# Attention scores and sums over keys as products of high and low fp32r parts, with query parts stacked on 128 rows

## The chip, the cores and the metric

The program runs on one core of one Trainium2 chip. The metric is the device time in microseconds (us), the median over runs. A core has the engines TensorE (PE; its weight loads are shown as PEld), VectorE (DVE), ScalarE (ACT), GpSimd (POOL) and SyncE (SP, which issues DMAs). Each takes its instructions in the order in which the program wrote them, and they meet at semaphores.

## What is computed

A diffusion block on 512 tokens and 256 context tokens of width 1024, then a second block with retention, gated linear attention and a product-key expert layer. The change touches the attention of the first block: 8 query heads over 2 key-value heads of width 64, for 512 queries and 768 keys (256 of them from the context).

```python
q, k, v, gb, gc, u = split_heads(px, q_norm[l], k_norm[l])      # rmsnorm of each head of q and k
a = latent_attention(apply_rope(q, cos, sin), apply_rope(k, cos, sin), v, kc, vc)
sc = gb * short_conv3(gc * u, conv_w[l])
mix = jnp.concatenate([rmsnorm(a, attn_out_norm[l]), rmsnorm(sc, conv_out_norm[l])], axis=-1)

def gqa_softmax(q, k, v):
    s = jnp.einsum('bqkgd,bskd->bkgqs', q, k, preferred_element_type=jnp.float32) * ATTN_SCALE
    p = jax.nn.softmax(s, axis=-1).astype(v.dtype)
    return jnp.einsum('bkgqs,bskd->bqkgd', p, v)
```

## The kernel before

Each engine has one hand-written list of steps, and this order by hand is the schedule; no planner stands behind it. PE writes into a ring of double banks of PSUM (`acc`) in numbered units. `begin(u)` waits until unit u-2 was freed, and ACT or DVE free a unit when they have read it (`acc_free`). Weights come in tiles of 128 x 1024: SP loads them, ACT copies out the high part (`high_part`, called through `ahead`), POOL subtracts (L2184), and each product of the projections is three fp32r products, high with high, high with low, low with high (L533 to L539). The attention of before doesn't do that: its products are plain fp32, and each shows as two matmul records in the trace.

**The projections of the mixing layer (L661 to L711).** PE computes q, k, v, then four tiles `gb`, four `gc`, four `u`, of 24 products of 512 columns each. Between the gate tiles lie the steps that make q and k ready: `stat` (L478, the mean of squares of each head, `blk64`), `rotated(t)` (L673, waits for `normed`, swaps pairs for the rotary embedding), `doubled_keys` (L680) and `to_tokens` (L658, v turned to tokens). For tile t, ACT squares, takes logarithm and exponential (`inverse`, each with a table load) to give `rstd`; DVE scales (L1728, `normed`), and after `rotated(t)` adds the rotary terms (`rope`, L1720 to L1722, `copied`). DVE does tile t wholly before tile t+1. ACT copies each gate tile out of PSUM (`gates`), so that a step which stands behind a `gates` in ACT's list can't begin before PE has finished that tile.

**The attention loop (L750 to L760; ACT L1254 to L1274; DVE L1751 to L1772).** A unit u is one head and 128 queries; there are 32. In step s PE does `scores(s+1)` (L724), `turn(s-2)` (L736, six transposes of the probabilities of a unit) and, every fourth step, `outputs(h)` (a product for the 512 queries of one head, shown as L478 into `misc`). ACT does the exponential of unit s with its row sum, then copies half of the turned unit s-3. DVE does the reciprocal of the sum of unit s-1 (L1756), scales that unit's probabilities (L1758), takes the row maximum of unit s (L1762) and its negative (L1763), and copies the other half of unit s-3 (L1771). Before a unit's exponential ACT needs DVE's L1763; before DVE's L1756 it needs the exponential. After the loop ACT and DVE norm the result and split it for the product with `w_mix_out`. POOL has nothing to do in the loop.

## Time and profile before

| what | us |
|---|---|
| median of 3 runs (3372.78 to 3380.73) | 3378.37 |
| profiled execution, its own time | 3377.58 |
| its span, first to last instruction | 3375.8 |
| PE busy in the span | 2841.4 (84%) |
| DVE, ACT, POOL busy | 1671.4, 951.1, 1072.3 |
| projections of the mixing layer from `gb`, up to the first scores | 731 to 811 |
| attention loop, to its last copy | 811 to 960 |

The page of the profile gives the busy time of each engine, the granted clock of TensorE by slices of the span, and the chain of work that ended last. Since a wait shows only at the engine that waits, one reads for each stage which engine has no idle time, and in a loop which ring of steps closes on itself. A busy time of PE is a bit too long for one product, because the records of pipelined products overlap; the distance from start to start is the true price. The granted clock is 1.00 (2.4 GHz) or 0.50 (1.2 GHz).

### The profile page before, as it was taken

How to read it: one execution, taken by the hardware profiler on the slowest of the kernel's cores; microseconds unless marked ns; L12 is line 12 of the kernel's file. 1: busy time of each engine (PE TensorE's matmuls, PEld its weight loads, DVE VectorE, ACT ScalarE, POOL GpSimd, SP SyncE). 2: the span in 40 equal slices, each digit the busy share in tenths (PEclk: the TensorE clock that was granted, in tenths of full speed). 3: DMA queues.
4: the chain of work that ended last, by engine and by line, in shares of the span. 5: the costliest groups of instructions: out<-in, count | busy, mean ns of one | idle time of the engine just before them, and what ended most of it. 6: DMA issues, size and time to landing. Idle time of an engine off the chain costs nothing.

```text
span 3375.8 us, 30023 instructions
## 1 busy us (share of the span) xinstructions
PE 2841.4 (84%) x11064; PEld 1915.0 (57%) x11064; DVE 1671.4 (50%) x3686; ACT 951.1 (28%) x1732; POOL 1072.3 (32%) x731
## 2 busy tenths in 40 slices
PE   6999989989988998989955688888877777777776
PEld 4999989866456887768823565444333333222322
DVE  3766640034525712120054435556777777776765
ACT  3111131144333223232133332223322222222221
POOL 1222222222013443323210024444544444444442
PEclk8999999988999999989967799999999999999999
DMA  4555522211004522212110028899999999999997
GB/s 191 174 178 176 180 66 62 66 60 53 0 25 150 187 88 88 88 44 69 39 38 1 13 89 319 341 356 418 420 427 427 427 427 427 427 427 427 427 427 307
DMA packets 126958, 722.13 MB, mean 214 GB/s; under 512 B 15204, under 2 KB 17516, under 8 KB 60140
## 3 DMA queue, kind: packets, MB, share of 16 engines
q0 software_dynamic: 73728, 536.90, 38.4%
q1 hardware_dynamic: 37448, 127.67, 11.1%
q10 hardware_dynamic: 15652, 55.90, 5.2%
q8 instruction: 73, 1.20, 0.1%
q14 instruction: 57, 0.47, 0.0%
HBM read 718.31 MB, written 2.10 MB: 213 GB/s over the span
## 4 chain that ended last, share of the span: by engine, by line
PE 60%; DMA 23%; DVE 9%; ACT 5%; issue 3%; POOL 0%; SPq 0%; DVEq 0%; ACTq 0%; POOLq 0%
PE acc L537 14%; PE acc L538 13%; PE acc L539 13%; DMA wring<-in_peer_rows,squares 7%; DMA hid<-in_peer_rows,squares 7%; PE sums L967 7%; DMA arena<-in_peer_rows,squares 4%; PE acc L967 3%; DMA resid<-in_peer_rows,squares 3%; PE sums L478 2%; PE misc L478 2%; ACT L1029 1%; DVE hid L1564 1%; DVE hid_parts L1570 1%; ACT hid L1029 1%
## 5 line engine op out<-in xcount | busy, mean ns | idle before, releaser
L2184 POOL TENSOR_TENSOR wring_parts<-wring,wring_parts 128x1024 fp32r<-128x1024 f32 (+1 forms) x215 | 515.6, 2409 | 1534.6 <-ACT wring_parts L1029 1534.3
L537 PE MATMUL acc<-hid_parts,wring_parts 128*128 128x384 f32 (+1 forms) x2128 | 791.8, 372 | 79.8 <-DVE hid_parts L1570 62.5
L539 PE MATMUL acc<-hid_parts,wring_parts 128*128 128x384 f32 (+1 forms) x2128 | 770.7, 362 | 0.0
L538 PE MATMUL acc<-hid_parts,wring_parts 128*128 128x384 f32 (+2 forms) x1696 | 615.6, 363 | 0.0
L537 PEld LDWEIGHTS acc<-hid_parts,wring_parts 128*128 128x128 f32 x2128 | 404.0, 190 | 155.7 <-issue 79.4
L539 PEld LDWEIGHTS acc<-hid_parts,wring_parts 128*128 128x128 f32 x2128 | 404.5, 190 | 38.4
L1029 ACT ACTIVATE wring_parts<-wring 128x1024 fp32r<-128x1024 f32 (+1 forms) x215 | 222.0, 1039 | 605.1 <-DMA wring<-in_w_ffn_out 223.0
L538 PEld LDWEIGHTS acc<-hid_parts,wring_parts 128*128 128x128 f32 (+1 forms) x1696 | 323.4, 191 | 31.6 <-issue 3.8
L2196 POOL DMA_INDIRECT arena<-in_peer_rows,squares x180 | 200.1, 1112 | 248.7 <-PE acc L967 137.3
L1029 ACT ACTIVATE hid<-hid 128x2 f32<-128x2 f32 (+2 forms) x292 | 65.5, 224 | 689.3 <-DVE arena L2075 221.6
L2196 POOL DMA_INDIRECT wring<-in_peer_rows,squares x158 | 169.9, 1076 | 219.2 <-PE acc L967 151.9
L538 PE MATMUL acc<-arena_parts,wring_parts 128*128 128x384 f32 (+1 forms) x656 | 239.4, 365 | 0.0
L1633 DVE TENSOR_TENSOR arena<-squares,acc 128x384 f32<-128x384 f32 (+1 forms) x66 | 39.5, 599 | 259.7 <-ACT squares L1029 259.7
L2196 POOL DMA_INDIRECT hid<-in_peer_rows,squares x109 | 117.6, 1079 | 158.6 <-PE acc L967 123.9
L1029 ACT ACT_TABLE_LOAD x124 | 159.1, 1283 | 9.5 <-issue 7.1
L1661 DVE SCALAR_TENSOR_TENSOR resid<-acc,halfg,resid 128x384 f32<-128x384 f32 (+3 forms) x32 | 16.2, 546 | 275.1 <-PE acc L539 275.1
L2075 DVE SCALAR_TENSOR_TENSOR arena<-arena,resid 128x1024 f32<-128x1024 f32 x101 | 124.0, 1228 | 26.7 <-DMA arena<-in_peer_rows,squares 26.3
L538 PEld LDWEIGHTS acc<-arena_parts,wring_parts 128*128 128x128 f32 x656 | 125.2, 191 | 15.4 <-issue 2.4
L2075 DVE SCALAR_TENSOR_TENSOR arena<-arena 128x1024 f32<-128x1024 f32 x79 | 97.0, 1228 | 61.0 <-DMA arena<-in_peer_rows,squares 59.9
L478 PE MATMUL sums<-squares,cst 128*128 128x384 f32 (+1 forms) x188 | 92.5, 626 | 39.3 <-ACT squares L1029 36.0
L1029 ACT ACTIVATE squares<-acc 128x384 f32<-128x384 f32 (+1 forms) x66 | 34.8, 527 | 314.5 <-PE acc L539 303.8
L2082 DVE TENSOR_TENSOR hid<-hid,squares 128x2 f32<-128x2 f32 x256 | 40.8, 160 | 165.1 <-ACT hid L1029 164.8
(357 smaller groups left out, 4392.0 us busy)
## 6 DMA issues: line engine op xcount, KB each, us to landing
wring<-in_w_ffn_in SPq DMA_DIRECT2D x88, 512.0 KB, 5.6
modw<-in_w_ada ACTq DMA_DIRECT2D x56, 512.0 KB, 4.0
modw<-in_w_mod ACTq DMA_DIRECT2D x48, 512.0 KB, 3.9
wring<-in_w_ffn_out SPq DMA_DIRECT2D x32, 512.0 KB, 3.5
wring<-in_w_in SPq DMA_DIRECT2D x28, 512.0 KB, 3.4
wring<-in_w_mix_in SPq DMA_DIRECT2D x18, 512.0 KB, 3.4
wring<-in_peer_w_q SPq DMA_DIRECT2D x16, 512.0 KB, 3.3
hid<-in_w_ada SPq DMA_DIRECT2D x6, 1024.0 KB, 17.1
```

What stands on the lines that cost most here:

```text
L478: return nc.tensor.matmul(o, w, x, start=(k == 0), stop=(k == last))
L537: nc.tensor.matmul(o, wh, high, start=first, stop=False)
L538: nc.tensor.matmul(o, wh, low, start=False, stop=False)
L539: return nc.tensor.matmul(o, wl, high, start=False, stop=last)
L967: mm = nc.tensor.matmul(o[:, hf, :], diag[n % N_DIAG], pair[PAIR_OF[n]][:, D + hf * 512:D + (hf + 1) * 512], start=(at == 0), stop=(at == ...
L1029: return nc.scalar.activation(o, i, func, **kw)
L1564: ins = V.scalar_tensor_tensor(low[:, j, lo:up_to], x[:, j, lo:up_to], gain[:, norm, j, c:c + 1], rstd[:, lo:up_to], ALU.mult, ALU.mult)
L1633: free(V.tensor_tensor(arena[:, (f * sides + hf) * width:(f * sides + hf + 1) * width], sg[:, (base + u) % 2, 0:width], acc[:, 2 * ((base ...
L2075: V.scalar_tensor_tensor(rows, rows, 1.0, xb[i // PEER_H], ALU.mult, ALU.mult, accum_out=p_dot[:, s:s + 1]).then_inc(dots_done, 1)
L2082: V.tensor_tensor(p_w[:, part], p_act[:, part], g_all[:, i * PEER_K + b * BATCH:i * PEER_K + (b + 1) * BATCH], ALU.mult).then_inc(weights_ ...
L2184: nc.gpsimd.tensor_tensor(Wlor[:, p, 0:blocks, 0:cols], Wlo[:, p, 0:blocks, 0:cols], Whir[:, p, 0:blocks, 0:cols], ALU.subtract).then_inc( ...
L2196: nc.gpsimd.indirect_dma_start(pair[PAIR_OF[n]], None, a["peer_rows"], bass.IndirectOffsetOnAxis(ap=idx_all[:, n:n + 1], axis=0)).then_inc ...
```

## The change

- **Queries.** After `rope` of tile t, ACT writes the high parts of its two heads, each on 64 rows, into `q_even[t]` and `q_odd[t]` (`q_highs(t)`, behind `gates` of gb2, gb3, gc0, gc1 in its list). DVE then waits for that, subtracts to get the low parts (`q_low`), PE moves these to the other 64 rows with a product (`swapped(t)`, four new units), and DVE copies them into place in the next round. So each head has its high part on one half of the rows and its low part on the other.
- **Keys and values.** `kdup` and `vtok` become a high part (ACT) and a low part (DVE subtracts from PSUM). The turning of v moves from behind gb3 to behind `doubled_keys(1)`.
- **Scores.** Two fp32r products of 128 rows with the high keys and two of 64 rows with the low keys, in place of two fp32 products of 64 rows.
- **Loop.** The scaling by the reciprocal moves from DVE to POOL. A turned unit is split: ACT copies the high part of both banks, DVE subtracts for the low part of both banks. `outputs` runs every second step for 256 queries: 18 fp32r products over all 128 columns of v, so both key-value heads are computed and one is used. The heads run in the order 1, 3, 5, 7, 0, 2, 4, 6; heads j and j+4 share a tile of the result, and rows of `w_mix_out` and of the norm's gains are permuted on the host to fit.

```diff
@@ -66,8 +67,9 @@
-                  ("gb0", 1), ("gb1", 1), ("rope_q0", 1), ("gb2", 1), ("rope_q1", 1), ("gb3", 1), ("vT", 1), ("rope_q2", 1),
-                  ("gc0", 1), ("rope_q3", 1), ("gc1", 1), ("rope_k", 1), ("gc2", 1), ("kdup0", 1), ("gc3", 1), ("kdup1", 1),
+                  ("gb0", 1), ("gb1", 1), ("rope_q0", 1), ("gb2", 1), ("rope_q1", 1), ("swap0", 1), ("gb3", 1), ("rope_q2", 1), ("swap1", 1),
+                  ("gc0", 1), ("rope_q3", 1), ("swap2", 1), ("gc1", 1), ("rope_k", 1), ("swap3", 1), ("gc2", 1), ("kdup0", 1),
+                  ("gc3", 1), ("kdup1", 1), ("vT", 1),
...
@@ -86,6 +88,7 @@
+HEAD_ORDER = (1, 3, 5, 7, 0, 2, 4, 6)
...
@@ -345,13 +356,16 @@
-        kdup, vtok = ar(2816, 2, TC), ar(4352, 6, P)
+        kdup_hi, kdup_lo = (arena_parts[:, at:at + 2 * TC].rearrange("p (a t) -> p a t", a=2) for at in (2816, 0))
+        vtok_hi, vtok_lo = (arena_parts[:, at:at + TC].rearrange("p (r n) -> p r n", r=6) for at in (4352, 15368))
+        q_even, q_odd = [modw_parts[:, T * t:T * (t + 1)] for t in range(4)], [arena_parts[:, 11272 + T * at:11272 + T * (at + 1)] for at in (1, 3, 0, 2)]
+        q_low = modrows[:, 0:T]
...
-        probT = hid[:, 0:KD * TC].rearrange("p (h r t) -> p h r t", h=2, r=6)
+        probT_hi, probT_lo = (hid_parts[:, at:at + 2 * 6 * 256].rearrange("p (h r t) -> p h r t", h=2, r=6) for at in (0, 3072))
...
-        v_features = ar(11272, TC)
+        v_features = ar(13320, TC)
...
@@ -681,6 +697,12 @@
+            def swapped(t):
+                b = begin(UNIT[f"swap{t}"])
+                pe.wait_ge(q_split, t + 1)
+                nc.tensor.matmul(acc[:, b, :], c_("swap_halves"), q_low, start=True, stop=True).then_inc(acc_ready, 1)
...
@@ -689,20 +711,24 @@
             stat(1, T, c_("blk64"))
             rotated(1)
+            swapped(0)
             gates(GB_UNIT, 3)
-            emptied(pe, UNIT["v"])
-            to_tokens(UNIT["vT"], v_features)
             stat(1, T, c_("blk64"))
             rotated(2)
+            swapped(1)
             gates(GC_UNIT, 0)
             stat(1, TC, c_("blk64"))
             rotated(3)
+            swapped(2)
             gates(GC_UNIT, 1)
             rotated(4)
+            swapped(3)
             gates(GC_UNIT, 2)
             doubled_keys(0)
             gates(GC_UNIT, 3)
             doubled_keys(1)
+            emptied(pe, UNIT["v"])
+            to_tokens(UNIT["vT"], v_features)
             feature_tile(UNIT["u"], s + 14, hi768r, lo768r)
             feature_tile(UNIT["u"] + 1, s + 15, hi768r, lo768r)
...
@@ -715,36 +741,44 @@
-                h, t = u // 4, u % 4
+                h, t = HEAD_ORDER[u // 4], u % 4
...
+                if u == 0:
+                    pe.wait_ge(q_stacked, 4)
...
+                q = (q_even, q_odd)[h % 2][h // 2][:, t * P:(t + 1) * P]
...
-                    mm = nc.tensor.matmul(acc[:, b + hf, 0:HALF], qT[rows, h // 2, t * P:(t + 1) * P],
-                                          kdup[rows, h // 4, hf * HALF:(hf + 1) * HALF], start=True, stop=True)
+                    nc.tensor.matmul(acc[:, b + hf, 0:HALF], q, kdup_hi[:, h // 4, hf * HALF:(hf + 1) * HALF], start=True, stop=False)
+                for hf in range(2):
+                    mm = nc.tensor.matmul(acc[:, b + hf, 0:HALF], q[rows, :], kdup_lo[rows, h // 4, hf * HALF:(hf + 1) * HALF],
+                                          start=False, stop=True)
...
-                if u:
-                    pe.wait_ge(probT_act, u)
-                    pe.wait_ge(probT_dve, u)
-                else:
+                if not u:
...
+                for bank in range(2):
+                    if u:
+                        pe.wait_ge(probT_dve, 2 * (u - 1) + bank + 1)
+                    for r in range(3):
+                        mm = nc.tensor.transpose(sums[:, bank, r * P:(r + 1) * P], prob[:, u % 3, (3 * bank + r) * P:(3 * bank + r + 1) * P], ident)
+                    mm.then_inc(probT_ready, 1)
+            def outputs(pair_of_units):
+                done, half = pair_of_units // 2, pair_of_units % 2
+                pe.wait_ge(probT_dve, 4 * (pair_of_units + 1))
+                if done and half == 0:
+                    pe.wait_ge(o_copied, done)
+                p = pair_of_units % 2
+                o = misc[:, 256 * half:256 * half + 256]
...
-                    mm = nc.tensor.transpose(sums[:, r // 3, (r % 3) * P:(r % 3 + 1) * P],
-                                             prob[:, u % 3, r * P:(r + 1) * P], ident)
-                mm.then_inc(probT_ready, 1)
-            def outputs(h):
-                pe.wait_ge(probT_act, 4 * (h + 1))
-                pe.wait_ge(probT_dve, 4 * (h + 1))
-                if h:
-                    pe.wait_ge(o_copied, h)
-                at, kv = 64 * (h % 2), h // 4
-                for r in range(6):
-                    mm = product(misc[at:at + 64, :], vtok[:, r, kv * HD:(kv + 1) * HD], probT[:, h % 2, r, :], r, 5)
+                    vh, vl = vtok_hi[:, r, :], vtok_lo[:, r, :]
+                    nc.tensor.matmul(o, vh, probT_hi[:, p, r, :], start=(r == 0), stop=False)
+                    nc.tensor.matmul(o, vh, probT_lo[:, p, r, :], start=False, stop=False)
+                    mm = nc.tensor.matmul(o, vl, probT_hi[:, p, r, :], start=False, stop=(r == 5))
...
@@ -756,8 +790,8 @@
-                if step >= 6 and (step - 6) % 4 == 0:
-                    outputs((step - 6) // 4)
+                if step >= 4 and step % 2 == 0:
+                    outputs((step - 4) // 2)
...
@@ -1223,27 +1257,40 @@
+            def q_highs(t):
+                act.wait_ge(copied, t + 1)
+                run(q_even[t][0:64, :], qT[0:64, t, :], ACT.Copy)
+                run(q_odd[t][64:128, :], qT[64:128, t, :], ACT.Copy).then_inc(q_high, 1)
...
+            q_highs(0)
...
-            u = UNIT["vT"]
-            b = unit(u)
-            run(vtok, wide(b, 6 * P).rearrange("p (r n) -> p r n", r=6), ACT.Copy).then_inc(acc_free[u % 2], 1)
+            q_highs(1)
...
+            q_highs(2)
...
+            def key_highs(kv):
+                b = unit(KDUP_UNIT[kv])
+                run(halves(kdup_hi[:, kv, :]), acc[:, b:b + 2, 0:HALF], ACT.Copy).then_inc(kv_high, 1)
...
+            q_highs(3)
...
-            take_unit(KDUP_UNIT[0], halves(kdup[:, 0, :]), cols=TC)
+            key_highs(0)
...
-            take_unit(KDUP_UNIT[1], halves(kdup[:, 1, :]), cols=TC)
+            key_highs(1)
+            b = unit(UNIT["vT"])
+            run(vtok_hi, wide(b, 6 * P).rearrange("p (r n) -> p r n", r=6), ACT.Copy).then_inc(kv_high, 1)
...
@@ -1256,22 +1303,24 @@
-                        act.wait_ge(probT_ready, step - 2)
+                        act.wait_ge(probT_ready, 2 * (step - 2))
...
-                    act.wait_ge(probT_ready, u + 1)
-                    if u >= 8:
-                        act.wait_ge(o_ready, u // 4 - 1)
-                    run(probT[:, (u // 4) % 2, 0:3, (u % 4) * P:(u % 4 + 1) * P],
-                        sums[:, 0, 0:HALF].rearrange("p (r n) -> p r n", r=3), ACT.Copy).then_inc(probT_act, 1)
+                    for bank in range(2):
+                        act.wait_ge(probT_ready, 2 * u + bank + 1)
+                        if u >= 4 and bank == 0:
+                            act.wait_ge(o_ready, u // 2 - 1)
+                        run(probT_hi[:, (u // 2) % 2, 3 * bank:3 * bank + 3, (u % 2) * P:(u % 2 + 1) * P],
+                            sums[:, bank, 0:HALF].rearrange("p (r n) -> p r n", r=3), ACT.Copy).then_inc(probT_act, 1)
...
-                    act.wait_ge(o_ready, h + 1)
-                    rows = slice(64 * (h % 2), 64 * (h % 2) + 64)
-                    run(mixT[rows, h // 2, :], misc[rows, :], ACT.Copy).then_inc(o_copied, 1)
+                    act.wait_ge(o_ready, 2 * (h + 1))
+                    head = HEAD_ORDER[h]
+                    rows = slice(64 * (head // 4), 64 * (head // 4) + 64)
+                    run(mixT[rows, head % 4, :], misc[rows, :], ACT.Copy).then_inc(o_copied, 1)
...
@@ -1729,6 +1778,25 @@
+                if t < 4:
+                    dve.wait_ge(q_high, t + 1)
+                    if t:
+                        dve.wait_ge(acc_ready, UNIT[f"swap{t - 1}"] + 1)
+                    V.tensor_tensor(q_low[0:64, :], qT[0:64, t, :], q_even[t][0:64, :], ALU.subtract)
+                    V.tensor_tensor(q_low[64:128, :], q_odd[t][64:128, :], qT[64:128, t, :], ALU.subtract).then_inc(q_split, 1)
+                if t >= 1:
+                    u = UNIT[f"swap{t - 1}"]
+                    b = unit(u)
+                    V.tensor_copy(q_even[t - 1][64:128, :], acc[64:128, b, :])
+                    free(V.tensor_copy(q_odd[t - 1][0:64, :], acc[0:64, b, :]), u)
+                    emptied(dve, u)
+                    dve.sem_inc(q_stacked, 1)
+            for i, (u, part, high) in enumerate([(KDUP_UNIT[kv], halves(kdup_lo[:, kv, :]), halves(kdup_hi[:, kv, :])) for kv in range(KV_HEADS)]
+                                                + [(UNIT["vT"], vtok_lo, vtok_hi)]):
+                dve.wait_ge(kv_high, i + 1)
+                b = unit(u)
+                src = acc[:, b:b + 2, 0:HALF] if i < 2 else wide(b, 6 * P).rearrange("p (r n) -> p r n", r=6)
+                free(V.tensor_tensor(part, src, high, ALU.subtract), u)
...
@@ -1753,9 +1821,8 @@
-                    free(V.reciprocal(inv, small[:, 2 + u % 2:3 + u % 2]), UNIT["scores"] + u)
-                    emptied(dve, UNIT["scores"] + u)
-                    V.tensor_scalar(prob[:, u % 3, :], prob[:, u % 3, :], inv, None, ALU.mult).then_inc(prob_ready, 1)
+                    V.reciprocal(inv, small[:, 2 + u % 2:3 + u % 2]).then_inc(sum_inverted, 1)
+                    dve.sem_inc(acc_free[u % 2], 1)
...
@@ -1765,11 +1832,11 @@
-                    dve.wait_ge(probT_ready, u + 1)
-                    if u >= 8:
-                        dve.wait_ge(o_ready, u // 4 - 1)
-                    V.tensor_copy(probT[:, (u // 4) % 2, 3:6, (u % 4) * P:(u % 4 + 1) * P],
-                                  sums[:, 1, 0:HALF].rearrange("p (r n) -> p r n", r=3)).then_inc(probT_dve, 1)
+                    for bank in range(2):
+                        dve.wait_ge(probT_act, 2 * u + bank + 1)
+                        at = slice((u % 2) * P, (u % 2 + 1) * P)
+                        V.tensor_tensor(probT_lo[:, (u // 2) % 2, 3 * bank:3 * bank + 3, at], sums[:, bank, 0:HALF].rearrange("p (r n) -> p r n", r=3),
+                                        probT_hi[:, (u // 2) % 2, 3 * bank:3 * bank + 3, at], ALU.subtract).then_inc(probT_dve, 1)
...
@@ -2211,8 +2278,16 @@
+            def scale_rows(u):
+                pool.wait_ge(sum_inverted, u + 1)
+                nc.gpsimd.tensor_scalar(prob[:, u % 3, :], prob[:, u % 3, :], small[:, 16 + u % 4:17 + u % 4], None, ALU.mult).then_inc(prob_ready, 1)
...
+                if s == TILE_OF["mix_out"] + W_RING - 1:
+                    for u in range(32):
+                        scale_rows(u)
...
```

## Rows read from the trace of the kernel before

**Rows 1.** The page: its span.

```profile
span 3375.8 us, 30023 instructions
```

**Rows 2.** Stretches: length, PE, PEld, DVE, ACT, POOL busy, PEclk, DMA share, GB/s.

```profile
731.00:811.00 80.00, 80.00 (x330) 61.05 (x329) 26.93 (x40) 43.62 (x51) 28.53 (x12) 1.00 0.24 79
...
820.00:848.00 28.00, 27.53 (x58) 13.51 (x59) 18.77 (x38) 8.84 (x19) 0.00 (x0) 0.50 0.00 1
848.00:959.00 111.00, 99.21 (x351) 45.20 (x349) 57.03 (x123) 38.51 (x82) 0.00 (x0) 1.00 0.00 0
```

**Rows 3.** Timeline of PE behind gb2: start, duration, instruction, [idle before].

```profile
749.95 1.02 PE L478 MATMUL sums<-squares,cst 128*128 128x512 f32 x2
750.81 1.02 PE L673 MATMUL acc<-arena,cst 128*128 128x512 f32 x2
```

**Rows 4.** Timeline of DVE around the same place.

```profile
747.55 0.75 DVE L1728 SCALAR_TENSOR_TENSOR arena<-arena,vec,rstd 128x512 f32<-128x512 f32 x1 [0.77 <-ACT rstd L1029]
751.92 0.69 DVE L1720 TENSOR_TENSOR arena<-acc,arena 128x512 f32<-128x512 f32 x1 [3.62 <-PE acc L673]
```

**Rows 5.** ACT: timeline of the copy of gb2; group of copies of 64 rows.

```profile
750.14 0.60 ACT L1029 ACTIVATE arena<-acc 128x512 f32<-128x512 f32 x1 [1.16 <-PE acc L539]
...
L1029 ACT ACTIVATE arena<-misc 64x512 f32<-64x512 f32 x8 | 4.7, 591 | 31.3 <-PE misc L478 31.3
```

**Rows 6.** Timeline of one steady step of the loop, all engines.

```profile
857.56 0.15 DVE L1763 TENSOR_SCALAR small<-small 128x1 f32<-128x1 f32 x1
...
857.75 0.90 ACT L1029 ACTIVATE hid<-acc,small 128x768 f32<-128x768 f32 x1 [1.56 <-DVE small L1763]
...
858.64 0.48 ACT L1029 ACTIVATE hid<-sums 128x384 f32<-128x384 f32 x1
858.77 0.16 DVE L1756 RECIPROCAL small<-small 128x1 f32<-128x1 f32 x1 [0.59 <-ACT hid L1029]
858.97 0.62 DVE L1758 TENSOR_SCALAR hid<-hid,small 128x768 f32<-128x768 f32 x1
...
859.22 0.84 PE L736 MATMUL sums<-cst,hid 128*128 128x128 f32 x6 [0.60 <-ACT hid L1029]
859.51 0.95 DVE L1762 TENSOR_REDUCE small<-acc 128x1 f32<-128x768 f32 x1
...
860.00 1.55 PE L724 MATMUL acc<-arena 64*128 64x384 f32 x4
```

**Rows 7.** Timeline of PE: the outputs of two heads at clock 1.00.

```profile
879.10 5.36 PE L478 MATMUL misc<-hid,arena 128*64 128x512 f32 x12
...
895.27 5.36 PE L478 MATMUL misc<-hid,arena 128*64 128x512 f32 x12
```

**Rows 8.** Timeline of PE in the first feed-forward: fp32r products of 384 columns.

```profile
559.87 0.33 PE L538 MATMUL acc<-arena_parts,wring_parts 128*128 128x384 f32 x1
...
560.04 0.33 PE L539 MATMUL acc<-hid_parts,wring_parts 128*128 128x384 f32 x1
```

**Rows 9.** Groups by form: subtractions of 384 columns on DVE, 768 on POOL.

```profile
L1650 DVE TENSOR_TENSOR arena_parts<-arena,hid_parts 128x384 fp32r<-128x384 f32 x32 | 15.1, 546 | 0.0
...
L2184 POOL TENSOR_TENSOR wring_parts<-wring,wring_parts 128x768 fp32r<-128x768 f32 x16 | 29.4, 1838 | 67.5 <-ACT wring_parts L1029 67.5
```

**Rows 10.** Timeline: one DVE scaling alone, one beside POOL.

```profile
793.49 0.49 DVE L1740 TENSOR_SCALAR arena<-arena,vec 128x512 f32<-128x512 f32 x1
...
797.17 2.40 POOL L2184 TENSOR_TENSOR wring_parts<-wring,wring_parts 128x1024 fp32r<-128x1024 f32 x1 [4.25 <-ACT wring_parts L1029]
...
798.93 0.92 DVE L1740 TENSOR_SCALAR arena<-arena,vec 128x512 f32<-128x512 f32 x1
```

**Rows 11.** Timeline of PE behind idle time, in two places.

```profile
962.60 6.40 PE L478 MATMUL sums<-squares,cst 128*128 128x512 f32 x8 [3.42 <-ACT squares L1029]
...
1703.36 1.10 PE L815 MATMUL acc<-arena,cst 128*128 128x512 f32 x2 [1.02 <-DVE tmp L1720]
1705.48 2.05 PE L815 MATMUL acc<-arena,cst 128*128 128x512 f32 x2 [1.02 <-DVE tmp L1720]
```

## What the change does to the time: a prediction

> **What bounds the kernel now.** I read the busy times by stretch first, then the timeline of PE, then those of the engines that PE waits for. The change touches two stretches that are bounded by different things. In the projections PE is the bound: 80.00 us busy of 80.00, at clock 1.00, from the first gate tile to the first scores [rows 2]. Whatever is put on PE's list there, or makes it wait, is paid in full. In the loop no engine is full. At clock 1.00 PE is busy 99 us of 111, and DVE and ACT far less [rows 2], yet a step takes 2.93 us. The reader can find the reason by following one ring in [rows 6]: negative maximum at 857.56, exponential at 857.75, reciprocal at 858.77, scaling at 858.97, maximum of the next unit at 859.51. DVE can't begin the next maximum before it has scaled the last unit, and it can't scale before ACT is done, so the latencies of two engines add up. PE's outputs stand outside that ring, 5.3 us for each head [rows 7], and from 879.10 to 895.27, from one head's outputs to the next [rows 7], four units take 16.2 us, 4.05 us each. The first 28 us of the loop run at clock 0.50 with PE full [rows 2]. The loop lasts from 811 to 959; PE can go on in it at 820, once the first exponential is done, so 139 us count from there.
>
> **The sum is made** against the profiled execution, 3377.58 us, of which 3375.8 are the span [rows 1]. The median of the runs shown is 0.8 us higher, and the forecast is set on it.
>
> **Part 1, the projections: new work on PE.** Four `swapped` products are fp32 with 512 columns, the form of `rotated`. A `stat` of the same form starts at 749.95 and the next product at 750.81 [rows 3], 0.86 us each: +3.4 us, on the path. Turning v is only moved.
>
> **Part 2, the projections: new waits.** This is the largest term, so here is its chain. PE's list has gb2, `stat`, `rotated(1)`. Before, DVE had scaled tile 1 at 747.55 [rows 4], while PE still worked on gb2, and `rotated(1)` followed `stat` without a gap at 750.81 [rows 3]. After, DVE stands in tile 0: behind its `rope` it waits for `q_high`, and ACT makes that only behind its copy of gb2. Queued behind that wait on DVE is the scaling of tile 1, and PE's `rotated(1)` waits for it. Counted from the end of gb2 at 749.95: ACT's copy starts at 750.14 and takes 0.60, two copies of 64 rows take 0.59 each [rows 5], so `q_high` stands at +2.0. Two subtractions at 0.69, the duration of the nearest form, `rope`'s product of 512 columns [rows 4], end at +3.4, the scaling of 0.75 [rows 4] ends at +4.2. PE gets there at +0.86, after `stat`: idle 3.3 us. In the next two rounds DVE also copies the two halves of the last `swapped` out of PSUM before it goes on, which I put at 0.62 each from the form of 0.60 to 0.69 above: idle 4.4 us, and 4.0 in the third, where the `stat` is one of 768 columns. In the fourth no `stat` stands between, and the scaling is one of 768 columns: 5.5 us. A last one of 1.2 us comes at the first u tile, whose bank is freed only by DVE's subtraction for the doubled keys, with just the turning of v as cover. Sum 18.4 us. I see no cover for it: the wait comes from the order of three lists, not from a slow engine. The bounds are 16 and 20 us, with the 64-row forms at 0.5 or 0.7 each.
>
> **Part 3, what the idle time does to the clock.** Where PE had waited 3.42 us, eight records of `stat` took 6.40 us [rows 11] in place of about 3.5 (four times 0.86), and the clock of that stretch was low. The four gaps here are of 3.3 to 5.5 us. Where a gap costs nothing the term is 0; at the 2.4 to 2.9 us of this row for each it is 10 to 12. I take 9, near the row, since the shortest gap may pass. The stage comes to 3.4 + 18.4 + 9 = +31 us, between +20 and +36.
>
> **Part 4, the loop: work on PE.** fp32r products of 384 columns start 0.17 us apart [rows 8]. Four of them make the scores 0.7 us in place of 1.5 (the record of 1.55 in [rows 6], less its overlap), 26 us less in 32 units. For 256 columns no row exists; from 0.17 at 384, less in proportion, 0.12, so that 18 take 2.1 us every second unit, 34 us in all in place of 8 x 5.3 = 42. The transposes stay at 0.8 [rows 6]. PE's work falls from 3.6 to 2.6 us a unit. This matters only if PE paces the loop, which brings us to the ring.
>
> **Part 5, the loop: the new ring.** DVE no longer scales, but subtracts for both banks of the unit turned before, and each subtraction waits for ACT's copy, which waits behind the next exponential in ACT's list. Follow it: negative maximum, exponential 0.90, two copies of 0.48 (pitch about 0.46), the second subtraction 0.53 to 0.55 (the form of 384 columns, [rows 9]), reciprocal 0.16, maximum 0.95, negative 0.15; all but the subtraction are of [rows 6]. With the gaps between engines that the same rows show, 0.1 or less each, that is 3.9 us (3.8 to 4.2). A unit took 4.05 on average. PE, at 2.6 us a unit, has room inside 3.9 us, so most of the 1 us that PE saves becomes idle time. Counted from 820: three units without subtractions and the convolution's norm, 7 us; 28 units at 3.9, 109 us; the last turns, copies and outputs, 12 us: 128 in place of 139, -11 us. POOL's scaling lies outside the ring. Its price is bounded by 0.62 (DVE's, [rows 6]) and 1.84 us (two inputs on POOL, [rows 9]); I take 1.0, below the two-input row, as it reads one input. The turn of that unit comes two steps later and covers either.
>
> **Part 6, the loop's clock.** The wait ahead of the loop (`inverse` with two table loads) is untouched, so I expect the same low start. There PE needs 4.8 us a unit for twice the work of part 4, and with waits up to 5.5; some five units at 1.0 to 1.6 more cost +5 us. Then the loop is left with -6. But at clock 1.00 PE would be busy 2.6 of 3.9 us, and in an uneven way: two pairs of turn and scores, one with outputs, and idle times of about 2.2 us. Before, it was busy 99 of 111 and the clock stayed [rows 2]. Elsewhere PE had 0.86 us of work in each 2.12 us, no wait over 1.02, and the clock still fell: the same two records took 1.10 us at 1703.36 and 2.05 us at 1705.48 [rows 11]. The new loop lies between these two. I hold it likelier that the clock falls and comes back many times: half of the units at 3.9 and half at 5.5 is 4.7, or 28 x 0.8 = 22 us on top of -11, so **+11 us**. Always low would be 28 x 1.6 = 45, so +34.
>
> **One rule weighed.** A DVE scaling of 512 columns took 0.49 us alone and 0.92 us when it began while POOL's subtraction was still running, and it ended just after that one [rows 10]. If DVE's small L1763 met POOL's new scaling in the same way, with that at its upper bound of 1.84 us, the maximum would end at 1.0 and L1763 would have to stay back until 1.9: 0.85 us in the ring, 28 x 0.85 = +24 us; at 1.0 us for the scaling it is nothing. The Trainium skill says this too: by "SBUF — State Buffer", section on the two separate sides, the pair of ports that GpSimd and VectorE share is an exclusive lock held for the whole instruction; by that rule the trace agrees, and only a one-column instruction is not shown there. The same skill's "GPSIMD Engine Reference", section 4.1, calls one-input work on GpSimd roughly line-rate, which would put the scaling near its lower bound.
>
> **The rivals.**
> (A) Stage stalls, loop with a changing clock: 3378.4 + 31 + 11 = 3420. For it: parts 2 and 6. Against it: the loop of before kept its clock.
> (B) The same stalls, the loop keeps its clock after the start: 3378.4 + 31 - 6 = 3403.
> (C) The same stalls, clock low nearly throughout: 3378.4 + 31 + 34 = 3443. PE is then full, and a full PE brought the clock back at 848 [rows 2]; that speaks against it.
> (D) POOL's scaling holds up L1763: 24 us on top of B, 3427.
> (E) The other side: faster. If DVE didn't bind, that is if subtractions and copies ran beside the exponential and not behind it, PE would pace the loop at 2.6 us, 28 x 1.3 = 36 us below the ring: 3403 - 36 = 3367. It decides where the ring falls below 3.5 us (from 3.9, 11 us) together with a stage term below +20. The lists forbid it as I read them.
> (F) The stalls of part 2 are hidden, because the copies for the queries come before the gate tile is done: +3 and -6, 3375, no change. The order of ACT's list speaks against it.
>
> **How the numbers follow.** A 0.43, B 0.26, C 0.12, D 0.09, E 0.06, F 0.04. The forecast is A's time, 3420. The bounds of A alone are 3408 to 3433. B with the stage at its lower bound, +20, gives 3392, and the upper half of C lies above 3445; leaving out E, F and that half of C leaves out less than 2 in 10, so 3391 to 3445. A measurement of this kernel can tell about 0.2% (6.8 us) from no change. Faster by more: E, 0.06. Within: F, 0.04. Slower: A to D, 0.90.
>
> **What would show it.** Right: PE idle four times, 3 to 6 us each, ahead of L673's product, ended by DVE's L1728, and the first scores some 30 us later than 811; DVE waiting for ACT behind `rope`; a distance of 3.9 us between exponentials where the clock is 1.00, with idle time on PE ended by DVE's subtraction; stretches of 0.50 inside the loop. Wrong: PE with no idle time between gb2 and gc2 (F); a loop clock of 1.00 from some 30 us after its start (B); L1763 far above 0.15 us (D); a distance below 3 us (E). The weakest step is the clock in part 6, because no stretch of before has PE busy in that share and pattern.

## The result, and the profile after

The changed kernel takes 3405.7 us (median of four runs, 3402.1 to 3408.0); the kernel before takes 3375.8 in runs beside them. The ratio is 1.0079, interval 1.0061 to 1.0098; in a second comparison, on another chip, it was 1.0071 (1.0054 to 1.0088). By these ratios the change costs 24 to 27 us; the quotient of the two medians, 1.0089, would be 30 us. The forecast was 3420, the range 3391 to 3445. Of the cases, rival B (3403: stalls in the projections, a loop that keeps its clock) came nearest, and the time lies between B and the forecast A.

The page's first two parts and the slices of the clock, to be held against [rows 1]:

```profile
span 3404.1 us, 30540 instructions
PE 2826.0 (83%) x11264; PEld 1940.2 (57%) x11264; DVE 1690.0 (50%) x3705; ACT 968.8 (28%) x1772; POOL 1148.8 (34%) x763
PEclk8999999988899999989967799999999999999999
```

The span is 28.3 us longer, and the busy shares say little of why. The stretches do (length, busy time and instructions of PE, PEld, DVE, ACT and POOL, the granted clock, the DMA share, GB/s), beside [rows 2]:

```profile
731.00:811.00 80.00, 59.63 (x209) 40.81 (x208) 29.96 (x39) 37.70 (x46) 17.52 (x8) 0.89 0.14 46
848.00:869.00 21.00, 12.98 (x33) 7.37 (x34) 10.30 (x24) 11.82 (x20) 11.33 (x6) 0.54 0.00 0
900.00:940.00 40.00, 31.85 (x197) 26.10 (x196) 22.05 (x53) 18.73 (x42) 22.26 (x11) 0.91 0.00 1
```

In the stretch in which PE had been busy 80.00 of 80.00 us it is now busy 59.63, at clock 0.89. PE's timeline shows where (start, duration, instruction, [idle before <- who ended it]):

```profile
755.70 1.10 PE L689 MATMUL acc<-arena,cst 128*128 128x512 f32 x2 [3.28 <-DVE arena L1777]
769.03 2.04 PE L689 MATMUL acc<-arena,cst 128*128 128x512 f32 x2 [4.81 <-DVE arena L1777]
784.90 2.03 PE L689 MATMUL acc<-arena,cst 128*128 128x512 f32 x2 [4.38 <-DVE arena L1777]
801.89 2.04 PE L689 MATMUL acc<-arena,cst 128*128 128x512 f32 x2 [7.90 <-DVE arena L1777]
821.00 0.53 PE L553 MATMUL acc<-hid_parts,wring_parts 128*128 128x512 f32 x1 [1.24 <-DVE arena_parts L1799]
```

L689 is the `rotated` product (two records for each), L1777 the scaling of the tile that it rotates, L1799 the subtraction for the doubled keys. These are the five stalls of part 2, 21.6 us in all. Behind the last three long ones the records of `rotated` are twice as long as at [rows 3]: 2.04 in place of 1.02. The first scores come at 844.31 in place of 810.67.

The loop, on the other hand, is shorter. One step of it, to be read like [rows 6] (L1063 is every ACT operation, L1838 DVE's subtraction of the high part, L1824 the reciprocal, L1829 and L1830 maximum and its negative, L2284 POOL's scaling, L767 the turn):

```profile
927.28 2.21 POOL L2284 TENSOR_SCALAR hid<-hid,small 128x768 f32<-128x768 f32 x1 [1.37 <-DVE small L1824]
928.20 0.15 DVE L1830 TENSOR_SCALAR small<-small 128x1 f32<-128x1 f32 x1
928.39 0.90 ACT L1063 ACTIVATE hid<-acc,small 128x768 f32<-128x768 f32 x1 [1.34 <-DVE small L1830]
929.29 0.86 ACT L1063 ACTIVATE hid_parts<-sums 128x384 fp32r<-128x384 f32 x2
929.80 1.02 DVE L1838 TENSOR_TENSOR hid_parts<-sums,hid_parts 128x384 fp32r<-128x384 f32 x2 [1.44 <-ACT hid_parts L1063]
930.50 0.92 PE L767 MATMUL sums<-cst,hid 128*128 128x128 f32 x6 [1.63 <-DVE hid_parts L1838]
930.81 0.94 DVE L1829 TENSOR_REDUCE small<-acc 128x1 f32<-128x768 f32 x1
930.99 2.21 POOL L2284 TENSOR_SCALAR hid<-hid,small 128x768 f32<-128x768 f32 x1 [1.50 <-DVE small L1824]
931.78 0.15 DVE L1830 TENSOR_SCALAR small<-small 128x1 f32<-128x1 f32 x1
931.97 0.90 ACT L1063 ACTIVATE hid<-acc,small 128x768 f32<-128x768 f32 x1 [1.82 <-DVE small L1830]
```

The reader sees the ring that was forecast (exponential, two copies, two subtractions, maximum, negative, exponential) with PE waiting 1.63 us on DVE; it takes 3.58 us, not 3.9. The next distance, of a step with outputs, is 3.71, and three times in the loop, about 30 us apart, one is 5.2. Those are the steps in which the clock falls. One of them lies in the middle of these three stretches (columns as above):

```profile
897.00:901.00 4.00, 2.37 (x17) 1.74 (x16) 2.53 (x6) 1.75 (x4) 2.50 (x2) 1.00 0.00 0
901.00:906.00 5.00, 5.00 (x28) 4.51 (x27) 1.98 (x6) 1.75 (x4) 3.63 (x2) 0.66 0.00 0
906.00:911.00 5.00, 3.37 (x26) 2.74 (x25) 2.57 (x7) 2.64 (x6) 1.98 (x2) 1.00 0.00 0
```

With the starts of the first and the last of the 32 exponentials as milestones, the 28 us of this execution add up:

| stretch | before | after | difference |
|---|---|---|---|
| span's start to first exponential | 818.8 | 854.1 | +35.3 |
| first to last exponential | 125.7 | 117.3 | -8.4 |
| last exponential to first product of `mix_out` (L537, L553) | 30.6 | 26.5 | -4.1 |
| from there to the end | 2400.7 | 2406.1 | +5.4 |

### The profile page after: what moved, and what is told of

It reads as the page before. It is cut to its first block, busy times and chain, and to the rows that moved or that the text cites. A ratio compares the mean times of both kernels' runs of the same rounds, so it can differ in the third digit from the quotient of the medians.

```text
span 3404.1 us, 30540 instructions
## 1 busy us (share of the span) xinstructions
PE 2826.0 (83%) x11264; PEld 1940.2 (57%) x11264; DVE 1690.0 (50%) x3705; ACT 968.8 (28%) x1772; POOL 1148.8 (34%) x763
## 4 chain that ended last, share of the span: by engine, by line
PE 34%; DMA 23%; DVE 7%; ACT 4%; issue 2%; POOL 0%; SPq 0%; ACTq 0%; DVEq 0%; POOLq 0%
DMA hid<-in_peer_rows,squares 7%; DMA wring<-in_peer_rows,squares 7%; PE acc L553 7%; PE acc L554 7%; PE acc L555 7%; PE sums L1001 6%; DMA arena<-in_peer_rows,squares 4%; DMA resid<-in_peer_rows,squares 4%; PE acc L1001 3%; PE sums L494 1%; ACT L1063 1%; DVE hid L1613 1%; ACT squares L1063 1%; DMA modw<-in_w_mod 1%; DVE hid_parts L1619 0%
## 5 line engine op out<-in xcount | busy, mean ns | idle before, releaser
L553 PE MATMUL acc<-hid_parts,wring_parts 128*128 128x384 f32 (+1 forms) x2128 | 793.8, 373 | 81.5 <-DVE hid_parts L1619 63.0
L553 PEld LDWEIGHTS acc<-hid_parts,wring_parts 128*128 128x128 f32 x2128 | 404.8, 190 | 160.5 <-issue 80.0
L1063 ACT ACTIVATE wring_parts<-wring 128x1024 fp32r<-128x1024 f32 (+1 forms) x215 | 222.2, 1040 | 608.1 <-DMA wring<-in_w_ffn_out 222.3
L1063 ACT ACTIVATE hid<-hid 128x2 f32<-128x2 f32 (+2 forms) x292 | 65.9, 226 | 689.2 <-DVE arena L2142 211.5
L1710 DVE SCALAR_TENSOR_TENSOR resid<-acc,halfg,resid 128x384 f32<-128x384 f32 (+3 forms) x32 | 16.2, 547 | 275.0 <-PE acc L555 275.0
L2142 DVE SCALAR_TENSOR_TENSOR arena<-arena,resid 128x1024 f32<-128x1024 f32 x101 | 124.3, 1231 | 26.8 <-DMA arena<-in_peer_rows,squares 26.5
L1063 ACT ACTIVATE squares<-acc 128x384 f32<-128x384 f32 (+1 forms) x66 | 34.8, 527 | 321.2 <-PE acc L555 294.1
L494 PE MATMUL sums<-squares,cst 128*128 128x384 f32 (+1 forms) x188 | 91.2, 617 | 40.6 <-ACT squares L1063 37.3
L2142 DVE SCALAR_TENSOR_TENSOR wring<-wring,arena 128x1024 f32<-128x1024 f32 x78 | 95.6, 1226 | 54.7 <-DMA wring<-in_peer_rows,squares 54.2
```

What stands on the lines that cost most here:

```text
L494: return nc.tensor.matmul(o, w, x, start=(k == 0), stop=(k == last))
L553: nc.tensor.matmul(o, wh, high, start=first, stop=False)
L1063: return nc.scalar.activation(o, i, func, **kw)
L1710: ins = V.scalar_tensor_tensor(x1, acc[:, b + bank, at:at + hi_ - lo], hgate[:, ffn, j, kind:kind + 1], x1, ALU.mult, ALU.add)
L2142: V.scalar_tensor_tensor(rows, rows, 1.0, xb[i // PEER_H], ALU.mult, ALU.mult, accum_out=p_dot[:, s:s + 1]).then_inc(dots_done, 1)
```

## The experiments

The same milestones for all kernels, in us. "Loop" is from the first to the last exponential, the distances are those behind the low start of the clock; PE's busy time is that of a stretch of 40 us at 900 (of 20 us with e8).

| kernel | ratio to before (interval) | first exp. | loop | distances in the loop | PE busy, clock |
|---|---|---|---|---|---|
| before | 1 | 818.8 | 125.7 | 2.93, 2.93, 2.93, 7.38 | 35.9, 1.00 |
| after | 1.0079 (1.0061 to 1.0098) | 854.1 | 117.3 | 3.58, 3.71, at times 5.2 | 31.9, 0.91 |
| e1, PE's order in the projections | 0.9977 (0.9967 to 0.9987) | 825.3 | 116.0 | 3.58, 3.71, at times 5.2 | 30.3, 0.96 |
| e2, ACT's copies first | 0.9981 (0.9968 to 0.9993) | 854.3 | 89.8 | 2.33, 3.42 | 39.4, 1.00 |
| e3, both | 0.9888 (0.9870 to 0.9906) | 825.4 | 89.3 | 2.33, 3.42 | |
| e4, fp32 scores | 0.9987 (0.9977 to 0.9998) | 818.4 | 121.8 | 3.58, 4.30, once 5.8 | 34.8, 0.97 |
| e5, more PE work in the loop | 1.0057 (1.0040 to 1.0074) | 852.3 | 116.5 | 3.57, 4.06 | 33.6, 1.00 |
| e6, DVE scales | 1.0104 (1.0087 to 1.0121) | 855.6 | 131.4 | 4.24, 4.24, at times 4.5 | 30.2, 0.91 |
| e7, before, POOL scales | 0.9983 (0.9973 to 0.9993) | 816.6 | 117.9 | 2.40, 2.61, 2.40, 7.91 | 38.1, 1.00 |
| e8, fp32 scores, copies first | 0.9918 (0.9901 to 0.9935) | 818.6 | 105.2 | 2.33, 4.38 | 20.0 of 20, 1.00 |
| e9, gaps filled late | 1.0093 (1.0077 to 1.0110) | 858.4 | 115.9 | 3.58, 3.71, at times 5.2 | 31.9, 0.96 |
| e10, after again | 1.0071 (1.0054 to 1.0088) | 854.6 | 116.3 | 3.58, 3.71, at times 5.2 | 31.0, 0.96 |
| e11, gaps filled | 1.0040 (1.0026 to 1.0054) | 851.3 | 117.0 | 3.58, 3.71, at times 5.2 | 31.9, 0.96 |

**e1: the order of three lists in the projections.** Each `swapped` stands one unit later on PE's list. DVE subtracts a round later and copies a round later, the last copies in the same round as before:

```diff
             rotated(1)
-            swapped(0)
             gates(GB_UNIT, 3)
...
             rotated(2)
-            swapped(1)
+            swapped(0)
...
+                    dve.wait_ge(q_high, t)
+                    if t >= 2:
+                        dve.wait_ge(acc_ready, UNIT[f"swap{t - 2}"] + 1)
+                    V.tensor_tensor(q_low[0:64, :], qT[0:64, t - 1, :], q_even[t - 1][0:64, :], ALU.subtract)
```

> The changed kernel with one thing moved: each swapped product stands one unit later on PE's list, DVE subtracts the query tile of the round before (after its own rope instead of waiting for ACT's fresh copy), and takes the swapped halves two rounds later. Same work, same products. Theory 1 (the stage's +32 us is four stalls made by the order of three lists, 3.3 + 4.8 + 4.4 + 7.9 us, plus the clock that falls behind each): the four gaps ahead of the rotated products go to under 1 us each, the first scores come 25 to 30 us earlier, the two doubled stat and rotated records return from 2.0 to 0.9 us, and the kernel takes 3376 to 3382 us. Theory 2 (the stage is longer because DVE and ACT have more to do than PE's units cover): gaps only move to other places, and the time stays above 3395 us. Theory 3 (stalls go, but the clock is low there for another reason): about 3387 us.

Measured 0.9977 to before, 32 to 34 us below the changed kernel (its ratios 1.0071 and 1.0079). PE in the stretch of the stalls, and three of its products (L494 is `stat`, L704 `swapped`):

```profile
731.00:811.00 80.00, 78.73 (x315) 57.89 (x315) 36.35 (x54) 46.51 (x57) 26.34 (x11) 1.00 0.22 73
757.53 1.02 PE L494 MATMUL sums<-squares,cst 128*128 128x512 f32 x2
758.39 1.02 PE L689 MATMUL acc<-arena,cst 128*128 128x512 f32 x2
759.24 1.02 PE L704 MATMUL acc<-modrows,cst 128*128 128x512 f32 x2
```

`rotated` follows `stat` without a gap, and nothing reappears elsewhere; the first exponential is 28.8 us earlier. The instructions are the same as in the changed kernel, so the stalls and what hangs on them were made by the order alone. Theory 1 holds, and its time was 3 us or more too high.

**e2: the copies ahead of the exponential on ACT.** The block of the exponential in ACT's loop is moved behind the two copies of the high part, nothing else (the lines left out between the two places are these copies):

```diff
-                if step < 32:
-                    u = UNIT["scores"] + step
-                    act.wait_ge(negmax_ready, step + 1)
...
+                if step < 32:
+                    u = UNIT["scores"] + step
+                    act.wait_ge(negmax_ready, step + 1)
```

> The changed kernel with ACT's list in the attention loop turned round: the high copies of the turned unit come before the next unit's exponential instead of behind it. Theory 1 (the distance of 3.6 us between exponentials is a ring: negative maximum, exponential, two copies, second subtraction, reciprocal, maximum): the copies, 0.86 us, leave the ring, the distance falls to about 2.9 us, and the kernel gains 15 to 22 us, to about 3386 us. Theory 2 (PE's 2.6 us a unit with its weight loads, or the granted clock, sets the distance): the distance stays above 3.4 us and the gain is under 5 us. If the clock falls less often because PE idles less, 3 to 5 us more.

Measured 0.9981 to before, 30 to 33 us below the changed kernel: more than the 15 to 22 us expected, and more than the 27 with the 5 us allowed for the clock. The loop is 27.6 us shorter:

```profile
906.45 0.87 ACT L1063 ACTIVATE hid_parts<-sums 128x384 fp32r<-128x384 f32 x2 [1.68 <-PE sums L767]
906.96 0.15 DVE L1830 TENSOR_SCALAR small<-small 128x1 f32<-128x1 f32 x1
907.03 1.01 DVE L1838 TENSOR_TENSOR hid_parts<-sums,hid_parts 128x384 fp32r<-128x384 f32 x2
907.21 0.91 ACT L1063 ACTIVATE hid<-acc,small 128x768 f32<-128x768 f32 x1
907.73 0.92 PE L767 MATMUL sums<-cst,hid 128*128 128x128 f32 x6
900.00:940.00 40.00, 39.35 (x267) 31.56 (x266) 30.63 (x70) 27.25 (x59) 30.59 (x15) 1.00 0.01 2
```

The subtractions now run at 907.03 beside the exponential at 907.21 and no longer behind it, and PE's next turn has no wait (only its weight load waits 0.38 us, for POOL's scaling). The distance falls from 3.64 to 2.88 us in the mean, and PE is busy 39.35 of 40 us at clock 1.00: with ACT's order turned round PE paces the loop, which it did not do in the changed kernel. The mean distance is 0.77 us shorter, 24 us over 31 distances; the remaining 4 us of the 27.6 would fit the steps at a lowered clock, which no longer occur behind the loop's start.

**e3: both.**

> Both edits together, the moved order in the projections and ACT's copies ahead of the exponential. If the two losses are independent their gains add: 24 to 29 us and 15 to 22 us, 3355 to 3366 us, below the kernel before. If they share the clock (a loop that starts at 2.4 GHz because the stage had no gaps) the sum is up to 6 us larger; if PE paces the loop once ACT's copies are out of the way, it stays at about 3375 us.

Measured 3343.8 us, 0.9888 to before: the first exponential of e1 (825.4) and the loop of e2 (89.3 us). The two losses are independent and their gains add. The time is 11 us below the range of 3355 to 3366, as each gain by itself was larger than expected. This kernel beats both others, by 1.1% and by 1.8 to 1.9%. The diff is that of e1 and of e2.

**e4: the split scores alone taken out.** Queries and keys stay fp32, there are no query parts and no `swapped`; probabilities and values are split and POOL scales:

```diff
-                    nc.tensor.matmul(acc[:, b + hf, 0:HALF], q, kdup_hi[:, h // 4, hf * HALF:(hf + 1) * HALF], start=True, stop=False)
-                for hf in range(2):
-                    mm = nc.tensor.matmul(acc[:, b + hf, 0:HALF], q[rows, :], kdup_lo[rows, h // 4, hf * HALF:(hf + 1) * HALF],
-                                          start=False, stop=True)
+                    mm = nc.tensor.matmul(acc[:, b + hf, 0:HALF], qT[rows, h // 2, t * P:(t + 1) * P],
+                                          kdup[rows, h // 4, hf * HALF:(hf + 1) * HALF], start=True, stop=True)
```

> The changed kernel with the scores as in the kernel before: fp32 products of queries and keys, no stacked query parts, no swapped products; only probabilities and values are split, and POOL scales. Theory 1 (the stage's loss belongs to the query and key parts alone, the loop's gain to probabilities, values and scaling): the first scores return to within 3 us of those before, the loop's PE work is 1.5 + 0.8 + 1.07 = 3.4 us a unit, just under the ring of 3.6 us, so the kernel takes 3372 to 3378 us, with a clock that no longer falls in the loop. Theory 2 (PE paces the loop again when the scores cost 1.5 us): distances of 4 us on average, 3380 us or more. Theory 3 (part of the 32 us stems from the values' parts or from elsewhere): first scores more than 6 us late.

The first exponential is back at 818.4: all of the +35 us ahead of the loop belongs to the query and key parts. In the loop the step with outputs takes 4.30 us in place of 3.71, so that there PE binds, and the step without them stays at 3.58, the ring. Theory 1's time holds (3377.1), its loop not quite: the mean is 3.94, near theory 2's 4. Nor did the clock stay up, as theory 1 had it: one distance is 5.82 in place of 4.30, and around it the clock is 0.79, with PE busy before and behind it as in the rest of the loop:

```profile
896.00:904.00 8.00, 6.96 (x32) 5.32 (x31) 3.21 (x9) 3.26 (x8) 4.53 (x3) 0.79 0.00 0
904.00:912.00 8.00, 6.97 (x40) 4.90 (x41) 4.43 (x11) 3.98 (x9) 3.01 (x3) 1.00 0.00 0
```

**e5: more work for PE in the loop.**

```diff
+                for hf in range(2):
+                    nc.tensor.matmul(acc[:, b + hf, 0:HALF], q, kdup_hi[:, h // 4, hf * HALF:(hf + 1) * HALF], start=True, stop=True)
                 for hf in range(2):
                     nc.tensor.matmul(acc[:, b + hf, 0:HALF], q, kdup_hi[:, h // 4, hf * HALF:(hf + 1) * HALF], start=True, stop=False)
```

> The changed kernel with the two score products of the high key parts issued twice in each of the 32 units (the first pair's sum is overwritten, so the output is the same): 0.34 us more work for PE a unit, 11 us in all. It tests whether PE has slack in the loop, and whether the 5.2 us distances (clock 0.66 to 0.69 for some 5 us, about every 30 us) come from PE's idle time. Theory 1 (DVE and ACT set the distance of 3.6 us, PE idles): the plain distances stay at 3.6 to 3.7 us, and at most 3 us are added where the clock is 0.50 or where outputs stand; if PE's higher share keeps the clock, three to four distances of 5.2 us go back to 3.6 us and the kernel is equal or up to 5 us faster. Theory 2 (PE paces the loop): +8 to +11 us.

```profile
869.00:900.00 31.00, 25.88 (x169) 21.35 (x169) 17.15 (x40) 13.95 (x32) 16.41 (x9) 0.98 0.00 1
900.00:940.00 40.00, 33.62 (x227) 27.96 (x226) 21.90 (x52) 20.44 (x47) 23.38 (x11) 1.00 0.01 1
```

All distances of 5.2 us are gone, and the clock is 1.00 where it was 0.91. The plain step stays at 3.57, the one with outputs grows from 3.71 to 4.06: in that step PE was already at its limit. Three falls at 1.5 us less, 12 such steps at 0.35 us more: the loop is as long as without the edit (116.5 against 117.3 and 116.3). So the added work took the falls away in this execution. The busy time alone doesn't explain them: PE was busy 33.6 of 40 us here, and 34.8 of 40 in e4, where one fall was left. PE has slack in every second step only, and 11 us of added PE work cost nothing (the kernel's ratio is even lower, but the intervals overlap).

**e6: the scaling back on DVE.**

```diff
+                    dve.wait_ge(sum_inverted, u + 1)
+                    V.tensor_scalar(prob[:, u % 3, :], prob[:, u % 3, :], inv, None, ALU.mult).then_inc(prob_ready, 1)
```

> The changed kernel with the scaling of the probabilities back on DVE, between reciprocal and maximum, as before the change. Theory 1 (the ring runs through DVE after ACT's copies): each unit pays the 0.62 us, the distance goes from 3.6 to 4.1 to 4.2 us, +15 to +19 us, and the clock falls more often, since PE idles more. Theory 2 (DVE isn't on the ring, ACT is): less than +5 us. POOL's 2.21 us a unit disappear in either case; if they had held up DVE, part of the 15 us comes back.

The distance is 4.24 us, 0.66 us more than the plain 3.58 and just above what theory 1 gave; the loop grows by 14.1 us. The whole kernel grows by 8 to 11 us by the ratios (1.0104 against 1.0079 and 1.0071), less than the 15 to 19 of theory 1; the profiled execution is 14.3 us longer than that of the changed kernel. So POOL's scaling is worth what it takes out of the ring.

**e7: POOL's scaling alone, on the kernel before.**

```diff
-                    V.tensor_scalar(prob[:, u % 3, :], prob[:, u % 3, :], inv, None, ALU.mult).then_inc(prob_ready, 1)
+                nc.gpsimd.tensor_scalar(prob[:, u % 3, :], prob[:, u % 3, :], small[:, 16 + u % 4:17 + u % 4], None, ALU.mult).then_inc(prob_ready, 1)
```

> The kernel before with one part of the change alone: POOL scales the probabilities; scores, turns and outputs stay as they were, all in fp32, no stacked parts. Theory 1 (the ring of before, negative maximum, exponential, reciprocal, scaling, maximum, 2.93 us, loses the 0.62 us of the scaling): it drops to 2.3 us, but PE's scores and turns take 2.3 us and its outputs 5.3 us a head, so PE becomes the bound at 3.6 to 3.7 us a unit in place of 4.05, -10 to -14 us. Theory 2 (PE already sets the pace, because its outputs stand in its list): under 3 us of gain. Theory 3 (POOL's 2.2 us a unit close the ring: scaled only 2.2 us after the reciprocal, and the turn waits for it): slower than before.

```profile
900.00:940.00 40.00, 38.13 (x136) 17.44 (x136) 17.84 (x41) 15.34 (x34) 24.23 (x11) 1.00 0.00 1
873.02 5.36 PE L479 MATMUL misc<-hid,arena 128*64 128x512 f32 x12
879.90 0.96 DVE L1762 TENSOR_REDUCE small<-acc 128x1 f32<-128x768 f32 x1 [5.54 <-PE acc L725]
```

The distances become 2.40, 2.61, 2.40 and 7.91, 15.3 us for four units in place of 16.2: the loop is 7.8 us shorter, the kernel 5.7 us (0.9983). Theory 1's direction holds, its size was about twice too large: I had put PE at 3.6 us a unit, and it is 3.8, busy 38.1 of 40 us. DVE waits 5.54 us for scores that stand behind the outputs. In the kernel before PE was thus close behind the ring; shorter ring, and PE binds.

**e8: fp32 scores and ACT's copies first.** The edits of e4 and of e2.

> Scores in fp32 as before (no stacked query parts, no swapped products), split probabilities and values, POOL's scaling, and ACT's copies ahead of the exponential. Its difference to the kernel with both edits is what the split scores are worth once the stalls and ACT's order are put right. Theory 1 (PE paces this loop: 1.5 for scores, 0.8 for turns, 1.07 for outputs a unit): mean distance 3.4 to 3.6 us in place of 3.9, 3358 to 3368 us, so that split scores gain some 15 us net of their 3.4 us in the projections. Theory 2 (the ring still binds at 3.9 us): no gain over the same kernel with the exponential first, about 3376 us.

PE is busy 20.00 of 20.00 us from 900 to 920, and the distance is 3.35 us in the mean: theory 1, with PE as the bound at 3.4. The kernel takes 0.9918 (3354.1 us, 4 us below the range expected). Against e3 (0.9888) the split scores are then worth 10 us, with 2 to 18 us by the two intervals together. The milestones give 9: 15.9 us in the loop, less the 6.8 us by which the first exponential comes later. That is the part of the change's promise that was real, 15 us expected.

**e9 and e11: work for PE in the gaps of the projections.** 3, 5, 4 and 8 products of constants stand ahead of the four `rotated` products that wait, in e9 behind `begin`, which waits for the bank, in e11 ahead of it:

```diff
+                for _ in range((0, 3, 5, 4, 8)[t]):
+                    nc.tensor.matmul(misc[:, :], c_("blk64"), cst[:, 0:T], start=True, stop=True, skip_group_check=True)
                 b = begin(ROPE_UNIT[t])
                 pe.wait_ge(normed, t + 1)
```

> The changed kernel with PE given work in its four gaps: ahead of the rotated products of tiles 1 to 4 stand 3, 5, 4 and 8 fp32 products of constants with 512 columns, written to a bank that nobody reads, 20 in all, 17 us of PE work at clock 1.00. The gaps of 3.3, 4.8, 4.4 and 7.9 us stay as long as they are, but PE is busy in them. Theory 1 (besides the idle time itself, the gaps let the clock fall, at 1.2 us for each of the pairs stat and rotated or rotated and swapped, in place of 0.9 us a product): the stage's clock is 1.00 throughout, the first exponential comes 5 to 10 us earlier than in the changed kernel, and the kernel takes 6 to 11 us less, 3392 to 3398 us. Theory 2 (the clock's part is small, the idle time is all): within 3 us of the changed kernel. Theory 3 (the extra products queue up ahead of the real ones): slower by 2 us or more.

```profile
765.89 6.12 PE L689 MATMUL misc<-cst 128*128 128x512 f32 x10 [3.82 <-DVE arena_parts L1793]
771.84 1.02 PE L691 MATMUL acc<-arena,cst 128*128 128x512 f32 x2
```

The fillers began 3.82 us into the gap, because PE first waits for its bank, which DVE frees at L1793, and they pushed `rotated` back. In my chain the gap had one wait at its end, the scaling; the trace shows that in the last three gaps most of it is a wait for the bank (3.82, 3.39 and 4.69 us), with the scaling behind. In the first one the bank was free. Theory 3 was right about the total (1.0093), though some 7 of the 8 us by which this kernel is longer than e10 arose behind the loop in the profiled executions (2408.0 us there against 2401.1). The run still told something: the three products were pushed back by 5.0, 2.5 and 5.3 us, 12.8 in all, and the first exponential came only 4.0 us later than in e10, both counted from the first `rotated`. The rest, 8.8 us, I put down to the clock: it is 0.96 from 731 to 811 us, in e10 0.83.

> The same 20 products of constants, 3, 5, 4 and 8 of them, but now ahead of both waits of each rotated product: the one for its bank, which DVE frees by the low parts of the last gate tile, and the one for the scaled tile. Placed between the two waits they had begun only when the bank was free, 3.4 to 4.7 us into the gap, and had pushed the real products back by some 13 us; the first exponential came only 4 us later than in the changed kernel, so that 9 us were given back by a clock of 1.00. Theory 1 (the clock's part is about 9 us): with the products from the gap's beginning on, the real ones are not pushed back by more than 2 us, the stretch from 731 to 848 us has the clock at 1.00, the first exponential stands at 845 to 848 us in place of 854.4, and the kernel takes 6 to 9 us less than the changed one (ratio to before 1.004 to 1.006). Theory 2 (those 9 us came from somewhere else): first exponential later than 851 us.

```profile
731.00:811.00 80.00, 76.66 (x274) 50.19 (x273) 28.10 (x40) 39.92 (x49) 19.02 (x8) 1.00 0.16 50
785.40 1.10 PE L691 MATMUL acc<-arena,cst 128*128 128x512 f32 x2 [0.94 <-DVE arena L1779]
```

With the fillers from the gap's beginning on, the clock is 1.00 throughout. The first exponential stands at 851.3 us all the same, outside the 845 to 848 of theory 1 and just where theory 2 begins. But this execution was 4.9 us later than e10 ahead of the stage already (its first `rotated` starts at 748.06, that of e10 at 743.14), so I count from there to the first exponential: 103.2 us against 111.5 in e10 and 109.1 in the changed kernel's first profile, 6 to 8 us less. The kernel takes 1.0040 against 1.0071 and 1.0079, 10 to 13 us less, although PE has 17 us more to do. Counted so, theory 1 holds: the clock's part of the stage is 6 to 10 us, besides the idle time.

**e10: the changed kernel again.**

> The changed kernel itself, unaltered, beside the one with filled gaps on the same chip. It tells whether three things seen in its one profile belong to the kernel or to that execution: first exponential at 854.1 us of the span, the distances of 5.2 us about every 30 us (four of them), and 4 us that arise only in the feed-forward stage behind the loop, where additions of DVE with two inputs take 2.9 in place of 0.75 us beside POOL. If they belong to the kernel: the same within 1 us each, ratio 1.006 to 1.010. If they are of the execution: one or more is missing, and the ratio is then nearer to 1.006 without the 4 us.

First exponential at 854.6, distances of 5.2 us three times (the expectation counted four), a loop of 116.3 us: these belong to the kernel. What arose behind the loop does not: from the first product of `mix_out` to the end it takes 2401.1 us, as before (2400.7), where the first profile had 2406.1. Over all executions here this stretch takes between 2399.7 (e2) and 2408.0 us (e9), in no order that I can see. A first `rotated` with the clock still up behind its gap (1.10, where e10 has 2.04) was of that execution, too.

## Why the prediction was right, and where its sizes were off

The sign, the order of the terms and the places were right, and the time 3405.7 lies inside the range. The forecast was 14 us too high, because two terms of the loop were mis-sized, by 22 us together. That the time is no further off is luck: 8 us that no term had, in the fourth gap and behind the loop, stood against them.

**Parts 1 to 3, the projections: right.** Forecast +31 us to the first scores; they come 33.6 us later. The parts: the four gaps and the one at the first u tile were to be 3.3, 4.4, 4.0, 5.5 and 1.2; they are 3.28, 4.81, 4.38, 7.90 and 1.24, 21.6 us in place of 18.4, which is above the bound of 20. Most of the miss is the fourth gap. DVE and POOL around it:

```profile
788.00 2.57 POOL L2251 TENSOR_TENSOR wring_parts<-wring,wring_parts 128x1024 fp32r<-128x1024 f32 x1 [12.58 <-ACT wring_parts L1063]
788.35 2.77 DVE L1771 TENSOR_TENSOR arena<-arena 128x512 f32<-128x512 f32 x1
797.94 0.68 DVE L1791 CAST arena_parts<-acc 64x512 fp32r<-64x512 f32 x1
798.60 2.34 POOL L2251 TENSOR_TENSOR wring_parts<-wring,wring_parts 128x1024 fp32r<-128x1024 f32 x1 [8.03 <-ACT wring_parts L1063]
798.77 2.98 DVE L1777 SCALAR_TENSOR_TENSOR arena<-arena,vec,rstd 128x768 f32<-128x768 f32 x1
```

L1777 for 768 columns takes 1.02 us elsewhere (at 773.17 in e1) and 2.98 here, where it begins 0.17 us behind POOL's subtraction and ends 0.8 us behind its end, as if it had waited for that end. In e1 the two meet as well, but DVE is 0.07 us ahead, and it is POOL's subtraction that grows, from 2.36 to 3.18 us:

```profile
773.17 1.02 DVE L1777 SCALAR_TENSOR_TENSOR arena<-arena,vec,rstd 128x768 f32<-128x768 f32 x1
773.24 3.18 POOL L2251 TENSOR_TENSOR wring_parts<-wring,wring_parts 128x1024 fp32r<-128x1024 f32 x1 [5.70 <-ACT wring_parts L1063]
```

I had weighed this meeting of the two engines for the loop, where it did not happen, and not for the projections, where it did. The Trainium skill says it in "SBUF — State Buffer", in the section on the two separate sides: the pair of ports that GpSimd and VectorE share is a lock held for a whole instruction by whichever of the two started first, and a VectorE instruction with two SBUF inputs is one of those that need it. By that rule the trace agrees, with 2.98 against 1.02.

The clock behind the gaps was taken at 9 us, and the comparison of e1 with the two profiles of the changed kernel gives 7.4 and 9.8: from the first `rotated` to the first exponential 109.1 and 111.5 us against 81.3, less the gaps of 20.4. Counted to the first scores only, it is 6.2 and 9.2; the rest is in the last part of this section. The gaps themselves were filled in e11, and 6 to 8 us came back. The bounds of 0 and 12 could have been drawn closer: [rows 11] was the right row.

**Part 4, PE's work: right.** fp32r products of 256 columns start 0.12 us apart, as estimated from those of 384. In e2, where PE paces, a unit takes 2.88 us; I had 2.6. The step with outputs was short of PE time already (e5), which the mean over two units had hidden.

**Part 5, the ring: right in kind, 0.3 us too long.** I had 3.9 us (3.8 to 4.2), it is 3.58 and 3.71. The durations that I listed add up to 3.64; the rest of the 3.9 were gaps between engines. The step shown above tells the difference. The two copies end 1.76 us behind the start of the exponential, where the sum had 1.84; the last subtraction ends 0.67 us behind them; the reciprocal, at 0.16 in the sum, costs nothing, since it overlaps the subtraction's end and the maximum's start; and the idle times between engines that I had added are in the durations already. Over 28 units that is 7 us. e2 takes the copies out of the ring and e6 puts the scaling into it, and the distance moves by -0.8 and +0.66 us: the ring was the bound.

**POOL's scaling: 2.21 us, outside of its bounds,** which ended at the 1.84 us of the two-input row [rows 9], and more than twice the 1.0 taken. This is where I was furthest off, and it had no consequence in this kernel: the turn comes two steps later. The Trainium skill's "GPSIMD Engine Reference", section 4.1, calls one-input work on GpSimd roughly line-rate; the trace disagrees: 2.21 us against 0.62 on DVE for the same form. Even this way rival D fails. L1830 takes 0.15 us at 928.20, while POOL's scaling of 927.28 still runs, and the maximum takes 0.94 at 930.81, beside the scaling of 930.99.

**Part 6, the loop's clock: the step that failed.** It said that the clock would fall and come back so often that half of the units take 5.5 us, 22 us in all. The clock does fall and come back, but seldom: three distances of 5.2 us in the loop, 1.6 us each over the mean of the others, 5 us. The low start costs 2 us, not 5: of the first six distances (21.7 us, and 22.0 before) only the sixth, 5.9 us, stands above the later pace, by 2.2 us. (Part 6 has PE at 4.8 us a unit there, for twice the work; twice the 2.6 us of part 4 is 5.2.) I had placed the loop between that of before and a row in which PE had 0.86 us of work in 2.12, and had then let it fall as often as that row. It was nearer to the loop of before. What sets how often the clock falls here stays open: e5 had no fall, and e4, with more PE time, had one.

Put 5 + 2 us where 22 stood, and take 7 off for the ring, and A's sum is 3420 - 15 - 7 = 3398, against the 3405.9 us of the profiled execution, of which 5 are from behind the loop and 3 are the gaps' excess. The kernel's loop is thus B's and not A's: its clock came back and, but for three short falls, stayed.

**The rivals.** B came nearest. C (clock low throughout) and F (stalls hidden) are refuted by the stretches, D by L1830. E said that PE would pace at 2.6 us if subtractions and copies ran beside the exponential, and that the kernel would then take 3367; the lists forbade it. e2 changed just this list, and took 3372. So E was a description of the better kernel, if with a pace of 2.88 us and not of 2.6.

**A term that I had not seen.** The first exponential follows the first scores by 9.8 us, where it was 8.1. Between them ACT makes squares, PE sums them (a `stat`), and ACT turns the sums into `rstd`. Before, the scores of 2.84 us stood ahead of that `stat`, and PE had waited 0.45 us for the squares when it took 1.13 us at 815.01. Now PE is done early, and ACT's squares come 0.9 us later behind the scores:

```profile
849.61 1.95 PE L494 MATMUL sums<-squares,cst 128*128 128x512 f32 x2 [1.69 <-ACT squares L1063]
```

The same records take 0.8 us more, on the chain that ends in the exponential. That part, of the clock, was of this execution: in e10 they take 1.12 us at 850.80, and the first exponential follows the first scores by 9.2 us. In both, the `stat` starts some 5.3 us behind the first scores, where it was 4.3; the squares stand behind ACT's copy of a weight tile, which waited 5.27 us for its DMA here and 5.32 in e10, but 4.85 before. e1, whose projections have no stalls, has part of this: counted from the first `rotated`, its first exponential comes 6.1 us later than in the kernel before, of which 3.4 + 1.2 are in the terms.

**What stays open.** Why the stretch behind the loop varies by 8 us between executions, and what sets how often the clock falls in the loop. e6's 8 to 11 us by the ratios against the 14 us that its loop lost need no cause: each of those ratios has an interval of some 6 us to either side.

## What to carry to other kernels

A cheaper product can be paid for twice by what its operands ask of the lists: here some 30 us of stalls and lowered clock came from where four products and their subtractions stood, and with the products one unit later on PE's list they were gone. Follow the ring of a steady loop and ask which of its members must be there; moving ACT's copies ahead of the exponential was worth 30 us, three times what the split of the scores saved. And before PE's time is cut, see whether PE is the bound: cut below it, the saved time becomes idle time, and idle time can cost clock on top.

## What the runs showed of the hardware

- 11 us of work on PE that nobody needs, 0.34 us a unit, cost nothing (e5), and 17 us of it in the projections made the kernel 10 to 13 us faster (e11). There the granted clock stayed at its level of 2.4 GHz (1.00), where it had fallen to 1.2 GHz (0.50) behind idle times of 3.3 (in e10, not in the first profile) to 7.9 us.
- In the loop the clock falls for a few us (0.66 over 5 us) two or three times, some 30 us apart. The falls recur in e1, e9, e10 and e11; e5, with more work on PE, has none behind its start, and e4 has one.
- A scaling of 128 x 768 fp32 elements with one column factor takes POOL 2.21 us, DVE 0.62.
- DVE's operations with both large inputs in SBUF (L1771, L1777) were held up by POOL, 0.7 and 1.0 us became 2.8 and 3.0; in e1, where DVE began first, POOL's subtraction became 3.18 us from 2.36; its subtractions with one input in PSUM and one in SBUF (L1838) were not, nor was the one-column L1830. In the timeline of e2 two of these subtractions lie wholly inside POOL's scalings (the record holds two in a row) and take 0.5 us each:

```profile
902.73 4.53 POOL L2284 TENSOR_SCALAR hid<-hid,small 128x768 f32<-128x768 f32 x2 [1.22 <-DVE small L1824]
903.66 1.01 DVE L1838 TENSOR_TENSOR hid_parts<-sums,hid_parts 128x384 fp32r<-128x384 f32 x2
```
